# Experts 8 to 27 of a 32-expert MoE step in one engine loop, with the down-bias products and sample rows moved from expert 16 to expert 28

## What is computed

```python
gate = softmax(top4(h @ router_w + router_b))
for each chosen expert e:
    u = h @ w_up[e] + b_up[e]                # 1024 -> 2048
    glu, lin = split(u); glu = min(glu, 7); lin = clip(lin, -7, 7)
    act = glu * sigmoid(1.702 * glu) * (lin + 1)
    y += gate[e] * (act @ w_down[e] + b_down[e])
x = x + g2 * y
out = rms_norm(x) * final_norm_g
```

## Time and profile before

| what | value |
|---|---|
| median of three runs | 1141.28 us (1140.9 to 1141.94) |
| the profiled execution's own time | 1141.32 us |
| its span in the profile | 1139.6 us |
| mean granted clock of TensorE | 0.991 of full |
| TensorE busy | 1098.8 us (96%) |
| VectorE / ScalarE / GpSimd busy | 416.2 / 187.0 / 25.0 us |
| DMA, moved in all | 460.42 MB, mean 404 GB/s |

### The profile page before, as it was taken

The page is one execution under the profiler, slowest core; times in us unless marked ns, Lnnn a source line. Parts: engine busy times, 40 slices in busy tenths (PEclk is TensorE's granted clock), DMA queues, the critical chain, the costliest instruction groups (busy, mean ns, idle before and its releaser), DMA issues.

```text
span 1139.6 us, 14866 instructions
## 1 busy us (share of the span) xinstructions
PE 1098.8 (96%) x6104; PEld 495.0 (43%) x6104; DVE 416.2 (37%) x871; ACT 187.0 (16%) x383; POOL 25.0 (2%) x57
## 2 busy tenths in 40 slices
PE   7999999999999999999999998999999999999996
PEld 5767678743334333333333333333333333333333
DVE  3157654343333333333323334333333333333333
ACT  1252223211111111111101011111111111111112
POOL 1100100000000000000000000000000000000002
PEclk9999999999999999999999998999999999999998
DMA  9988959999999999999999999999999999999993
GB/s 377 417 330 321 363 198 377 362 397 414 430 400 428 428 426 434 433 430 433 428 431 432 429 434 430 433 429 434 430 428 435 426 436 428 435 429 426 428 427 156
DMA packets 33529, 460.42 MB, mean 404 GB/s; under 512 B 5088, under 2 KB 6112, under 8 KB 12096
## 3 DMA queue, kind: packets, MB, share of 16 engines
q1 hardware_dynamic: 27808, 448.33, 93.2%
q0 software_dynamic: 2688, 9.47, 2.4%
q10 hardware_dynamic: 2976, 1.81, 0.5%
HBM read 454.94 MB, written 4.65 MB: 403 GB/s over the span
## 4 chain that ended last, share of the span: by engine, by line
PE 77%; DMA 20%; DVE 1%; issue 0%; ACT 0%; POOL 0%; DVEq 0%; SPq 0%; ACTq 0%
PE bank L1494 32%; PE bank L1550 15%; DMA ring<-in_w_up 13%; PE bank L1108 7%; PE bank L1537 5%; PE bank L1467 4%; DMA ring<-in_w_last 3%; PE bank L1362 3%; PE bank L1514 3%; DMA ring<-in_w_ada 1%; PE bank L1476 1%; DMA arena<-sample_values 1%; PE bank L1069 1%; PE bank L1525 1%; PE bank L1704 1%; DMA sample_values<-ring 1%
## 5 line engine op out<-in xcount | busy, mean ns | idle before, releaser
L1494 PE MATMUL bank<-ring,arena 128*64 128x512 f32 x2016 | 449.6, 598 | 14.4 <-DMA ring<-in_w_up 14.3
L1494 PEld LDWEIGHTS bank<-ring,arena 128*64 128x64 f32 x2016 | 141.5, 138 | 310.6 <-issue 286.2
L1550 PE MATMUL bank<-ring,arena 128*64 128x512 f32 x960 | 212.7, 595 | 0.0
L1550 PEld LDWEIGHTS bank<-ring,arena 128*64 128x64 f32 x960 | 66.6, 137 | 124.7 <-issue 123.8
L1108 PE MATMUL bank<-arena,ring 128*128 128x264 f32 x448 | 106.4, 391 | 0.7 <-DVE arena L1813 0.7
L2196 DVE COPY arena<-bank 128x512 f32<-128x512 f32 x32 | 22.1, 692 | 191.2 <-PE bank L1494 191.2
L918 ACT ACTIVATE arena<-bank 128x512 f32<-128x512 f32 x32 | 19.2, 599 | 435.5 <-PE bank L1494 435.5
L1108 PEld LDWEIGHTS bank<-arena,ring 128*128 128x128 f32 x448 | 82.8, 190 | 17.7 <-issue 4.3
L2250 DVE TENSOR_TENSOR arena<-bank,arena 128x512 f32<-128x512 f32 x31 | 21.4, 692 | 187.4 <-PE bank L1550 187.4
L1537 PE MATMUL bank<-arena,gpickT 64*128 64x512 f32 x240 | 76.7, 628 | 0.0
L2245 DVE TENSOR_TENSOR arena<-arena,bank 128x512 f32<-128x512 f32 x120 | 74.2, 680 | 0.0
(11 more groups left out here) (348 smaller groups left out, 691.6 us busy)
## 6 DMA issues: line engine op xcount, KB each, us to landing
ring<-in_w_up SPq DMA_DIRECT2D x41, 4096.0 KB, 29.0
ring<-in_w_up SPq DMA_DIRECT2D x43, 2048.0 KB, 14.3
ring<-in_w_down SPq DMA_DIRECT2D x21, 4096.0 KB, 26.7
ring<-in_w_down SPq DMA_DIRECT2D x18, 2048.0 KB, 13.1
ring<-in_w_ada SPq DMA_DIRECT2D x24, 1024.0 KB, 9.7
ring<-in_w_in SPq DMA_DIRECT2D x12, 1024.0 KB, 11.7
ring<-in_w_o SPq DMA_DIRECT2D x4, 1024.0 KB, 9.8
arena<-in_w_up SPq DMA_DIRECT2D x5, 512.0 KB, 19.7
```

The source lines that it names most:

```text
L1494: last = mm(bank[64 * half:64 * half + 64, b, :], xe[:, par, k % 4, k // 4, :], src[:, 512 * half:512 * half + 512], start=(k == 0), stop= ...
L1550: last = mm(bank[64 * half:64 * half + 64, b, :], acts[:, k, :], src[:, 512 * half:512 * half + 512], start=(k == 0), stop=(k == KT - 1))
```

## The change

MIDDLE_AT goes from 16 to 28, and the loops of experts 8 to 15 and 20 to 27 with the straight experts 16 to 19 between them become one loop of five rounds of four. What each expert does, the order of the loads and the waits are as before; the bias stage, the sample rows and the waits that belong to them (in `experts(act)`, `experts(pe)` and `experts(dve)`, in `add_up` and `take_rows`) now stand at expert 28, in the straight code behind the loop.

```diff
 PEEL, UNROLL = 8, 4
-MIDDLE_AT = 16
-LOOPS = (MIDDLE_AT - PEEL) // UNROLL
-LATE = 2
+MIDDLE_AT = 28
+LOOPS = (NE - 2 - PEEL) // UNROLL
...
     with eng.Fori(0, LOOPS) as q:
         for r in range(PEEL, PEEL + UNROLL):
             yield q * UNROLL + r, r, q
-    for n in range(MIDDLE_AT, MIDDLE_AT + UNROLL):
-        yield n, n, 0
-    with eng.Fori(0, LATE) as q:
-        for r in range(MIDDLE_AT + UNROLL, MIDDLE_AT + 2 * UNROLL):
-            yield q * UNROLL + r, r, q
-    for n in range(MIDDLE_AT + UNROLL + LATE * UNROLL, NE - 2):
+    for n in range(PEEL + LOOPS * UNROLL, NE - 2):
         yield n, n, 0
```

## The result

The changed kernel takes 1150.28 us in the median of six runs (1148.83 to 1150.65), the kernel before beside it 1141.73 us; the ratio is 1.0068 with a 95% interval of 1.0055 to 1.0081. The profiled executions are 1148.93 us (span 1147.2) and 1141.32 us (span 1139.6), 7.6 us apart.

What follows compares the result with a forecast made beforehand. TensorE and DMA were both taken as full, with transfers setting the pace wherever TensorE waits. From 1141.32 us, + 14.81 for the stage at 28 - 2.22 covered = + 12.59, so 1153.9 us; range 1150.5 to 1156.5.

Steps and rivals of the forecast that it cites:

- The stage at 16 gives nothing when it goes.: Expert 16: removing the stage's 14.81 us gains 0, since TensorE would wait for DMA instead.
- It costs 14.81 us at 28.: Expert 28, near 1044 us: the same products and waits take 14.81 us of TensorE's time.
- the clock rival: Stage at 28: low clock falls on the down products, 1155.2 us, or lasts as long again, 1158.7 us; 10%.
- 2.22 us of it are covered.: Behind the stage at 28: TensorE's two waits for DMA, 0.88 and 1.34 us, hide 2.22 us.
- The transfers before it are neither fewer nor sooner.: Transfers up to expert 27's second half: the queue never ran dry, so their gain is 0.
- The bound: Experts 16 to 27: if the stage caused their slower transfers, expert 28 would begin 1.6 us earlier; kept for the range.
- Back edges cost nothing.: Loops: no gap at the first loop's back edge, so going from two back edges to four adds 0.
- 14.8 us less leave about 20 us: SyncE's last issues: 35.05 us of queued transfers shrink to about 20 us, so the queue does not run dry.
- The neutral case: Experts 16 to 27: TensorE is the bound, so expert 28 loses what 16 gains; 1141.7 us, 4%.
- the dearer stage: Stage at 28: costs more through low clock on the down products, 1155.2 us, or a longer low clock, 1158.7; 10%.
- the late weights: Kernel's end: SyncE's issues fall 14.8 us behind and the last weights land later than 1129.9 us; up to 1156.0 us, 2%.
- The range's low end: 1150.5 us, taking in nearly both cheaper cases together: earlier transfers (-1.6 us) and a clock that stays up (-2.2 us).

Runs made afterwards that it cites:

- the second comparison: The changed kernel itself measured once more beside the kernel before (1141.97 us): 1152.00 us, ratio 1.0082.
- Experiments 1 and 3: 1: kernel before, old loops kept, only the stage moved to expert 28: 1154.43 us. 3: kernel before with the stage left out: 1139.48 us.
- experiment 5: Against the kernel before: one loop of three rounds (experts 8 to 19), then ten straight experts with the stage at expert 20: 1140.32 us, ratio 0.9975.

## Why the prediction was right and wrong

Its sign held, and so did its main mechanism: the stage is hidden at expert 16 and lies open at 28. Its size was too large, 12.6 us against 8.6 and, in the second comparison, 10.0. Between the two profiled executions 5.0 us are missing: 2.1 for the pause at the end, 1.6 for the faster stream of weights, 0.8 of scatter and 0.5 of waiting that hid more than I summed. Two steps failed: the gain of the transfers, taken as 0, and the tail, taken as unchanged.

- *The stage at 16 gives nothing when it goes.* Right: without it the last weights landed 0.16 us from where they had, and TensorE's waits for DMA grew from 14.3 to 29.7 us. The small change of time there is the pause.
- *It costs 14.81 us at 28.* Right in the first profile (14.8); 16.0 in the second, inside what the clock rival allowed for.
- *2.22 us of it are covered.* Somewhat short: from landing to `down_last` the path grew by 12.1 us and not 12.59. The profile's idle times run from modelled ends of products that overlap the next start; so the two waits of 0.88 and 1.34 us can have been longer, and 14.8 - 12.1 = 2.7 us were hidden.
- *"The transfers before it are neither fewer nor sooner."* This step failed. They were sooner by 1.6 us. The bound stood in the text, but I took 0 for it and gave the gain, if any, to the lag behind the stage. Experiments 1 and 3, without the lag, lost the same 1.5 us, and so did experiment 5, where straight code follows the loop. So the gain came with the single loop, which loads no code in that stretch; that the loads are the cause is not shown. Expert 28's gather began at 1029.07 us, where I had expected 1031.4 and named anything before 1029 as a sign of being wrong.
- *The pause at the end* is no step of the prediction at all, and this is the larger omission: the change of the tail stood at nothing, and the tail became 2.1 us shorter. It was in the order of time that I read for `down_last`, as "issue", a few rows further on. I took the tail behind the last weights as unchanged because its instructions are. No other wait of TensorE's products in that profile has that cause. It moves with code that is never executed, so a change of loops may move it too; why it went altogether is not shown.
- *Back edges cost nothing.* Right. The rule of the Trainium skill ("Runtime: NRT & Kernel Launch", section "Instruction fetch mechanics") spoke of a stall at a taken branch. The loop's back edges show none, and from 561 to 1040 us no code was loaded at all: the body stayed in. The jump over the overflow branch near the end is where a load of instructions and a pause stand close together. The trace agrees with the rule only in part there: in the kernel before one product runs between the jump and the pause, and in the changed kernel a load stands at the same product without a pause. Still, that branch was the one to weigh, and I did not.
- *"14.8 us less leave about 20 us" of queue.* At the end of the kernel that was right: the last weights, issued at 1094.58 and 1098.01, landed some 20.5 us later, and TensorE came for them at 1127. As a rule it would have misled: at expert 6 the queue held 14 us and ran dry, at expert 11 nearly so.
- *The neutral case, the dearer stage, the late weights.* The first and the third did not come. The second came in part, 1.2 us in one of two profiles, and there it made up for part of the two missed terms; that the second measurement, 1152.0 us, comes nearer to 1153.9 is in part such luck.

The two missed terms point the same way. The range's low end allowed for 3.4 us below the forecast; the faster stream and the pause together are 3.7, and the pause, over half of that, was allowed for nowhere.

## What to carry to other kernels

Work of TensorE that waits on other engines is free under a stream of weights only inside a window: late enough that the queue of issued loads is longer than the work, early enough that the experts behind it pay the lag off, here 14.8 us at about 2 us an expert. Here experts 16 and 20 lie in it, 11 just inside with a thin queue, 6 and 28 don't, and 24 is on its edge. Read both sides before moving such work: the time from issue to landing there, and the waits for transfers behind it. And when a change alters the length or the loops of a program, look in the tail for waits with cause "issue": the one here moved with the code's length and came or went with the loops.

## What was not expected of the hardware

- Just behind a jump over code that isn't executed, TensorE lost 2.1 us at the end of the kernel before, between the first and the second of four products. Adding code inside the jump moved the pause ahead of all four. A load of instructions stands there too (16 KB: 41 of them are 0.67 MB on the page), but the changed kernel has it as well, without the pause.
- A stretch with eleven loads of code, 0.15 MB, lost 1.5 us in a stream of 206 MB, in the kernel before all of it at one landing (11.2 us instead of 9.7) beside two of the loads, while the other nine delayed nothing. A loop of four experts loaded nothing after its first round.
- The same stage of short products took 14.8 to 17.4 us: 14.8 and 16.0 in two executions of one kernel, 16.0 at expert 6, 16.1 at 11, 17.4 at 20 and 24, by how long the clock stayed at 1.2 GHz and on which products. The Trainium skill ("TensorE: Matmul & The Clock Gate", section "What's actually happening") calls the window of the clock gate free-running; the two profiles of the changed kernel agree with that, since the clock fell about 2 us earlier in the stage in the second one.
